# A row of gains loaded once and spread by TensorE in place of a spreading load, and x tiles loaded between two halves of a weight

## What is computed

```python
def rmsnorm(x, g):
    y = xf * lax.rsqrt(jnp.mean(xf * xf, axis=-1, keepdims=True) + RMS_EPS)
    return (y * g.astype(jnp.float32)).astype(x.dtype)

    h = rmsnorm(x, pre_g)
    p = jnp.einsum('btd,de->bte', h, w_in)
    ...                                    # windowed and differential attention, gates
    y = jnp.einsum('bte,ed->btd', jnp.concatenate([ya, yb], axis=-1), w_out)
    return x + rmsnorm(y, post_g)
```

## Time and profile before

| | us |
|---|---|
| median of 3 runs | 531.4 |
| lowest and highest | 531.16, 531.54 |
| span of the profiled execution, first to last instruction | 529.6 |
| TensorE busy in it | 511.7 |
| VectorE, ScalarE, GpSimd busy | 269.9, 250.5, 105.8 |

### The profile page before, as it was taken

How to read it: one execution, slowest core, us unless ns; L and a number is a source line. 1 busy time by engine, 2 the same in 40 slices (tenths; PEclk the granted TensorE clock), 3 DMA queues, 4 the chain that set the end, 5 groups by cost and what they waited for, 6 DMA issues and landing times.

```text
span 529.6 us, 7514 instructions
## 1 busy us (share of the span) xinstructions
PE 511.7 (97%) x2776; PEld 424.8 (80%) x2776; DVE 269.9 (51%) x650; ACT 250.5 (47%) x614; POOL 105.8 (20%) x91
## 2 busy tenths in 40 slices
PE   6899999999999999999988999999999999999995
PEld 6799997888878887888875666678788887888884
DVE  3656002465675566445446687656555385443332
ACT  5454213466476466556565675644454463221211
POOL 3410303030112110212033243222201252000000
PEclk9999999999999999999999999999999999999998
DMA  8730005130101110110111010111000653332222
GB/s 295 228 123 2 1 15 143 41 74 6 40 10 33 40 41 0 41 40 9 34 41 27 14 41 1 40 41 41 0 1 0 144 176 120 102 132 84 80 79 79
DMA packets 41300, 32.57 MB, mean 61 GB/s; under 512 B 18544, under 2 KB 35888, under 8 KB 41264
## 3 DMA queue, kind: packets, MB, share of 16 engines
q1 hardware_dynamic: 38960, 27.89, 18.7%
q10 hardware_dynamic: 2304, 4.20, 2.1%
HBM read 27.40 MB, written 4.19 MB: 60 GB/s over the span
## 4 chain that ended last, share of the span: by engine, by line
PE 85%; ACT 4%; DVE 4%; issue 3%; DMA 2%; POOL 2%; SPq 0%; DVEq 0%; POOLq 0%; ACTq 0%
PE proj L1164 39%; PE scores L1263 14%; PE proj L1134 10%; PE scores L1183 7%; PE banks L1204 6%; PE banks L1194 3%; PE scores L1228 2%; PE banks L1246 2%; PE banks L1236 1%; PE scores L1107 1%; DVE k_stack L961 1%; DMA pre_g<-in_pre_norm_g 1%; DMA w_raw<-in_w_in 1%; ACT k_stack L762 1%; PE banks L1213 1%
## 5 line engine op out<-in xcount | busy, mean ns | idle before, releaser
L1164 PE MATMUL proj<-hT_hi,w_hi 128*128 128x512 f32 x336 | 90.0, 401 | 0.8 <-DVE k_stack L961 0.6
L1164 PE MATMUL proj<-hT_lo,w_hi 128*128 128x512 f32 x336 | 90.6, 402 | 0.0
L622 POOL TENSOR_TENSOR w_lo<-w_raw,w_hi 128x1024 fp32r<-128x1024 f32 x21 | 51.0, 2430 | 195.4 <-ACT w_hi L711 195.4
L1164 PE MATMUL proj<-hT_hi,w_lo 128*128 128x512 f32 x336 | 89.2, 400 | 0.0
L1164 PEld LDWEIGHTS proj<-hT_hi,w_hi 128*128 128x128 f32 x336 | 60.3, 188 | 15.0 <-issue 1.9
L1164 PEld LDWEIGHTS proj<-hT_hi,w_lo 128*128 128x128 f32 x336 | 60.8, 188 | 13.7 <-issue 1.9
L1164 PEld LDWEIGHTS proj<-hT_lo,w_hi 128*128 128x128 f32 x336 | 59.9, 188 | 13.2 <-issue 1.9
L1016 DVE CUSTOM_DVE_ANT_0 weights<-scores,dist_b 128x128 f32<-128x128 f32 (+7 forms) x64 | 45.9, 755 | 47.2 <-PE scores L1183 47.0
L782 ACT ACTIVATE weights<-weights,small 128x128 f32<-128x128 f32 (+7 forms) x64 | 49.0, 767 | 14.0 <-DVE small L1016 14.0
L792 ACT ACTIVATE weightsT<-banks 128x512 f32<-128x512 f32 (+3 forms) x48 | 23.5, 490 | 51.4 <-PE banks L1194 51.4
L1183 PE MATMUL scores<-k_stack,q_stack 128*128 128x512 f32 (+3 forms) x192 | 41.9, 353 | 0.0
(11 more groups left out here) (106 smaller groups left out, 724.7 us busy)
## 6 DMA issues: line engine op xcount, KB each, us to landing
w_raw<-in_w_in SPq DMA_DIRECT2D x13, 512.0 KB, 3.9
x_in<-in_x SPq DMA_DIRECT2D x8, 512.0 KB, 5.5
w_raw<-in_w_in SPq DMA_DIRECT2D x16, 256.0 KB, 3.6
x_res<-in_x SPq DMA_DIRECT2D x8, 512.0 KB, 4.4
out<-y_out ACTq DMA_DIRECT2D x16, 256.0 KB, 2.2
wv_raw<-in_w_in SPq DMA_DIRECT2D x2, 640.0 KB, 7.4
wo_early<-in_w_out SPq DMA_DIRECT2D x4, 256.0 KB, 4.5
w_raw<-in_w_out SPq DMA_DIRECT2D x4, 256.0 KB, 6.5
```

Of the source, the lines that this page charges most:

```text
L622: nc.gpsimd.tensor_tensor(w_lo[:, n % SPLIT], w_raw[:, n % RAW], w_hi[:, n % SPLIT].bitcast(F32), ALU.subtract).then_inc(w_lo_ready, 1)
L1164: last = nc.tensor.matmul(to, w[:, slot, k, :], h[:, k, HALF * half:HALF * half + HALF], start=(p == 0 and k == first), stop=(p == PIECES ...
```

## The change

- The 512 KB load of `pre_g` is gone from SP. ACT issues a load of the one row (`gain_row`, 1 x 1024, 4 KB) as its first instruction.
- POOL sets a row of 128 ones (`ones_row`) ahead of its other constants.
- PE multiplies: a column of 128 outputs, each 1.0 times the gain row, in two float32 matmuls of 512 columns with one row of depth, one for each bank of `proj`. They stand in the warm-up loop behind its ninth transpose, behind a wait for the row's load; the other 15 transposes follow. The warm-up now writes to `scores`.
- DVE copies the two halves out of `proj` to `pre_g` ahead of everything else that it does.
- SP's order becomes: x tile 0, v weights first half, x tile 1, v weights second half, x tile 2, and then as before.

```diff
             load_x(0)
-            sp.dma_start(pre_g[:, :], pre_norm_g[0:1, :].to_broadcast([P, D_MODEL])).then_inc(pre_g_loaded, 16)
             for part in range(2):
                 k = slice(4 * part, 4 * part + 4)
                 sp.dma_start(wv_raw[:, k, 0:VG], w_cols[:, k, BV:BV + VG]).then_inc(wv_loaded[part], 16)
-            load_x(1)
-            load_x(2)
+                load_x(1 + part)
...
+            nc.gpsimd.memset(ones_row[:, :], 1.0).then_inc(ones_made, 1)
             nc.gpsimd.memset(neg_half, -0.5).then_inc(half_made, 1)
...
+            act.dma_start(gain_row[:, :], pre_norm_g[0:1, :]).then_inc(gain_loaded, 16)
             square_x(0)
...
             def norm_x(t):
-                if t == 0:
-                    dve.wait_ge(pre_g_loaded, 16)
                 dve.wait_ge(x_scaled, t + 1)
-                for k in feature_parts(t):
+                for part, k in enumerate(feature_parts(t)):
+                    if t == 0:
+                        dve.wait_ge(pre_g_ready, part + 1)
...
+            for half in range(2):
+                dve.wait_ge(gain_spread, half + 1)
+                nc.vector.tensor_copy(pre_g[:, HALF * half:HALF * half + HALF],
+                                      proj[:, half, :]).then_inc(pre_g_ready, 1)
             norm_x(0)
...
-            for _ in range(WARM_UP):
-                nc.tensor.transpose(proj[:, 1, 0:P], ident[:, :], ident[:, :])
+            for turn in range(WARM_UP):
+                nc.tensor.transpose(scores[:, 1024:1024 + P], ident[:, :], ident[:, :])
+                if turn == WARM_UP // 3:
+                    pe.wait_ge(ones_made, 1)
+                    pe.wait_ge(gain_loaded, 16)
+                    for half in range(2):
+                        nc.tensor.matmul(proj[:, half, :], ones_row[:, :], gain_row[:, HALF * half:HALF * half + HALF],
+                                         start=True, stop=True).then_inc(gain_spread, 1)
             turn_x(0)
```

More of the change, by code:

```diff
@@ L275, in hybrid_layer @@
     lam_in = place("lam_in", 118, [P, 4, HEAD_DIM])
+    gain_row = place("gain_row", 192, [1, D_MODEL])
+    ones_row = place("ones_row", 116, [1, P])
     wo_hi = place("wo_hi", 96, [P, KT, D_MODEL], F32R)
@@ L336, in hybrid_layer @@
     wo_loaded = [sem(f"wo_loaded{i}") for i in range(WO_RAW)]
-    pre_g_loaded = sem("pre_g_loaded")
+    gain_loaded = sem("gain_loaded")
+    ones_made = sem("ones_made")
+    gain_spread = sem("gain_spread")
+    pre_g_ready = sem("pre_g_ready")
     post_g_loaded = sem("post_g_loaded")
@@ L486, in wait_proj_free @@
         if before < 0:
+            engine.wait_ge(pre_g_ready, before + 3)
             return
```

## The result

| | before | changed |
|---|---|---|
| median of the runs, us | 531.4 | 535.1 |
| lowest and highest | 531.16, 531.54 | 534.66, 535.29 |
| span of the profiled execution | 529.6 | 533.5 |
| TensorE busy in it | 511.7 | 517.1 |

The ratio is 1.0066, with a 95% interval of 1.0053 to 1.0078: slower by 3.7 us. The forecast was 532.8 in a range of 531.3 to 534.0, so the sign was right and the size was not: 1.45 us were forecast, and the result lies above the range.

What follows compares the result with a forecast made beforehand. TensorE, busy 97%, bounds the kernel; only its start is open. Low-level gain matmuls, the second copy and the remaining transposes move tile 0's turning from 7.31 to 8.76: 531.4 + 1.45 = 532.8 us, range 531.3 to 534.0.

Steps and rivals of the forecast that it cites:

- What bounds the kernel: TensorE bounds; only the start is open, where a delay d of tile 0's turning (7.31) reaches tile 2's turning (18.39) whole.
- The removal is worth at most 0.2 us: Tile 0's norm, at 6.51, could start at about 6.31 without the 512 KB load, as POOL's root ends at 6.28.
- The price of a matmul: Each one-row float32 gain matmul of 512 columns on TensorE costs 1.81 us at the low level, 0.90 at the upper.
- The row lands in time: The gain row on ACT's queue lands at 2.9 us, before nine transposes end at 3.53, so TensorE does not wait.
- Copies and POOL's memset: DVE's second copy from PSUM takes 0.69 us, ending at 7.93; POOL's extra memset delays TensorE's start by 0.05 us.
- The level rises between 6.5 and 7.3 us: TensorE goes from 1.2 to 2.4 GHz in the warm-up, taken at 6.9; the 15 later transposes then take 1.64 us.
- the 0.09 of slack: Ahead of tile 0's turning, the 15 transposes end at 8.67 us, just under the norm path's 8.76.
- Two side sums on other moments of the rise: Delay of tile 0's turning if TensorE's level rises elsewhere: at 6.0 d = 0.9 us, at 8.4 d = 1.9 us.
- Rival 2: TensorE's level stays low behind the one-row matmuls, the 15 transposes take 3.24 us: d = 3.5, 534.9 us; chance 0.10.
- The order of the loads is worth 0: On the load queue, earlier landings and the other order of x tiles gain 0, being covered by ACT's own work.

Runs made afterwards that it cites:

- depth_1: Kernel before, its 512 KB gains load kept, plus two unread float32 matmuls one row deep behind the ninth warm-up transpose, waiting for no load: 535.0 us, ratio 1.0063.
- gain_9: Changed kernel without the 15 warm-up transposes behind the gain matmuls; the nine ahead of them stay: 533.6 us, ratio 1.0039.
- after_order: Changed kernel with x tiles 1 and 2 loaded behind both halves of the v weights again, as before: 535.3 us, ratio 1.0067.
- order_only: Kernel before with SP's new order of loads alone, the 512 KB gains load kept: 532.2 us, ratio 1.0017.
- split_9: Changed kernel without the 15 transposes behind the gain matmuls, and DVE copies and norms the first half before copying the second: 532.2 us, ratio 1.0011.

## Why the forecast missed

- **What bounds the kernel.** Right. The shift at tile 0's high part arrived unshortened at tile 2's turning (3.72 us both) and at the end.
- **The removal is worth at most 0.2 us.** Nothing contradicts it: tile 0's square still starts at 4.11, against 4.12 in the earlier trace rows, so the removed load held up nothing ahead of it. No run tests the limit itself, since wherever the load is gone tile 0's norm waits for a copy; 0.2 us could not be told from no change.
- **The price of a matmul.** Right: 3.71 us for the pair where 3.62 was forecast, at the lower level.
- **The row lands in time.** Right. The matmuls start 3.79 - 1.68 = 2.11 us behind the first transpose, in depth_1, which waits for no load, 3.66 - 1.55 = 2.11 us.
- **Copies and POOL's memset.** The copy takes 0.69 us as forecast; the memset delays TensorE's start by 0.14 us (1.54 to 1.68), not 0.05, since it took 0.19 us and not the 0.10 of its neighbours. The second copy came at 7.60 where 7.2 was forecast, the norm's start at 8.21 where 7.96 was, and tile 0 could have been turned at about 9.0, as in gain_9, instead of 8.76.
- **The level rises between 6.5 and 7.3 us.** This is the step that failed. I took the moment of the rise from the trace of a kernel that ran transposes without a gap and carried it over to one in which half of that time goes to matmuls one row deep. From forecast to result at tile 0's high part there are 2.27 us (11.85 against 8.76 + 0.82). The fifteen transposes took 3.25 us, from 7.50 to 10.75, and not 1.64: 1.61. The four turning transposes and the step to ACT took 1.10 and not 0.82: 0.28. The matmuls ended at 7.50 and not 7.03, which counts 0.38 behind the 0.09 of slack: of the 0.47 between 7.03 and 7.50, 0.12 is again the rise that I had put at 6.9, 0.09 the price of the pair, and 0.26 the later start of TensorE with a pause of 0.17 us ahead of the first matmul. The forecast was 2.3 us short at the end. Two side sums on other moments of the rise were also slightly off: by the same steps a rise at 6.0 gives d = 1.0 and not 0.9, one at 8.4 gives 2.1 and not 1.9. None of them reaches 3.7; only a level that stays low through the fifteen transposes does.
- **The rivals.** Rival 2 described this mechanism and priced it at 534.9; 535.1 was measured. It had a chance of 0.10 and lay outside the range. Its price was worked out from rows, but its chance was set by a feeling that TensorE's clock would treat any busy instruction alike. No row showed a matmul one row deep, which is a reason to hold both levels open for the fifteen transposes, and the range should have reached to 535.
- **The order of the loads is worth 0.** Right for the changed kernel (after_order), wrong as a statement about the order alone (order_only): the cover that I named, ACT's own work, is too short for it when the gains' 512 KB stay in the queue. Without them it suffices in split_9, and in the changed kernel tile 0's delay covers it besides.

## What to carry to other kernels

A chain of waits that runs through TensorE's warm-up has the clock's level in it: before something is put among warm-up instructions, price what stands behind it at both levels, and count shallow matmuls as work that may not let the level rise. If they must be there, let what matters stand ahead of them and let each consumer wait for its own half: here dropping the fifteen transposes and splitting the copies gave back 2.9 of 3.7 us. And a load whose landing is named by the chain is worth at most its distance to the next condition of the same instruction, by the rows of the kernel before 0.2 us here.

## What the runs showed of the hardware

- With two float32 matmuls of 1, 32 or 64 rows by 512 columns among the transposes, TensorE ran at 1.2 GHz until after 10.6 us; with the same at 128 rows, of ones or of zeros, it ran at 2.4 GHz by 7 us. Whether the lower level would rise under shallow matmuls that go on longer wasn't tried.
- The granted clock is given as 1.00 from the start although the pace of the transposes is that of 1.2 GHz until the first rise; in gain_9 eight projections still take 2.33 us from 14.92 us on, with 1.00 recorded. The falls that it records later fit the pace: in the changed kernel it gives 0.50 from 16 to 19 us, behind a stretch from 12 us on in which TensorE stood half of the time, and eight projections take 2.33 us there instead of 1.33. This second low stretch is off the chain and costs nothing. It isn't fixed to the program either: in after_order TensorE works and stands in the same way from 13 to 16 us, and the clock stays at 1.00. The rows of the changed kernel:

```profile
15.00:16.00 1.00, 0.61 (x4) 0.90 1.04 341
16.00:17.00 1.00, 1.00 (x5) 0.50 0.98 288
17.00:18.00 1.00, 1.00 (x5) 0.50 0.01 2
```

- The moment of the first rise isn't fixed to the program. The same 24 transposes, in kernels whose first 7 us on TensorE are alike, took 5.38 us in the profile before and 4.65 us in order_only's timeline:

```profile
1.55 4.65 PE L1139 MATMUL proj<-ident 128*128 128x128 f32 x24 [1.55 <-POOL ident L630]
```
